# Order of the high-half and low-half products in the feed-forward loop of a two-model transformer kernel

## The chip, the core and the metric

The kernel runs on one core of a Trainium2 chip. The metric is the device time of one execution in microseconds. The median of three runs stands for a kernel. A core has TensorE for matrix products (results go to PSUM, which has eight banks of 512 float32 columns per partition), VectorE, ScalarE, GpSimd, and SyncE, which here issues the loads of the weights.

## What is computed

Two small transformer stacks follow each other on a sequence of 256 tokens with 1024 features. Each has two layers; every layer has a mixer and one or two feed-forward stages. The change lies in the feed-forward stages, of which there are six in all:

```python
def _swiglu(x, wg, wu, wd):
    return (jax.nn.silu(x @ wg) * (x @ wu)) @ wd
...
    for l in range(DEPTH):
        g = norm_g[l]
        h = _swiglu(_rmsnorm(x, g[0]), ffn_w_gate[l, 0], ffn_w_up[l, 0], ffn_w_down[l, 0])
        x = x + 0.5 * _rmsnorm(h, g[1])
...
        h = _swiglu(_rmsnorm(x, g[4]), ffn_w_gate[l, 1], ffn_w_up[l, 1], ffn_w_down[l, 1])
        x = x + 0.5 * _rmsnorm(h, g[5])
```

The weights are float32: gate and up are 1024 x 2816, down is 2816 x 1024. The second stack has one such stage per layer.

## The kernel before

Precision comes from splitting. ScalarE rounds every weight piece (128 x 2048) to a high half `w_hi`, VectorE makes the low half `w_lo = raw - w_hi`, and the activations are split in the same way: `xt[:, kb, 0:256]` is the high half of the transposed input for feature block `kb`, `xt[:, kb, 256:512]` the low half. A product is the sum of three: high by high, high weight by low input, low weight by high input. Because the two halves of `xt` lie side by side, one matmul of 512 columns with a block of `w_hi` standing gives the first two at once, into the two halves of a PSUM bank, and a matmul of 256 columns with `w_lo` standing gives the third, into the first half of the same bank. ScalarE and VectorE add the two halves of the bank afterwards.

A feed-forward stage walks over 11 chunks of 256 hidden features. A chunk has three weight pieces: two for gate and up together (feature blocks 0 to 3 and 4 to 7) and one for down. Each piece lands in one of three slots (`raw`, `w_hi`, `w_lo`), and the slot of a piece is free for the next when the product has used it (`piece_used`).

The first chunk and the last are written out. The eight between run in the hardware loop `with pe.Fori(2, NC - 1, 2) as c`, whose body holds two calls of `step`, so two chunks. One `step` is `gate_up` for chunk c and then `down` for chunk c - 1. In `gate_up` the loop path (no `banks` given) runs over two halves; each half waits once for its piece (`split`) and then goes over four feature blocks `kb`. For one feature block there are four column blocks `b` of 128 (two of gate, two of up), each with its own PSUM bank `GU_LOOP + b`: L1598 is the product of 512 columns, L1601 that of 256. The last instruction of a half raises `piece_used`. `down` is 24 matmuls of 512 columns (L1512, through `threes`).

Around it, a chunk's products are waited for by ScalarE, which copies the second halves of the four banks (L729), and VectorE, which adds the first halves (L1132) and scales the sum (L1136); this frees the banks for the next chunk (`up_scaled`). TensorE runs its instructions in the order in which they are written; no scheduler moves them. Six stages with eight chunks each are 48 passes through a `step`, with 32 matmuls of L1598 and 32 of L1601 in each.

In the profile, a weight load is a row of its own (PEld, LDWEIGHTS) under the line of its matmul.

Of the kernel before, what the change touches and what calls it, by code (L numbers as in the profile page):

```python
# [160 lines left out]
def program(nc, A, out):  # L161
# [5 lines left out]
    with ExitStack() as ctx:  # L167
# [1327 lines left out]
        def _(pe):  # L1495
# [9 lines left out]
            def threes(group, stands="x"):  # L1505

                for n, (hi_lo_a, hi_lo_b) in enumerate(((0, 0), (1, 0), (0, 1))):
                    for o, xh, xl, wh, wl, start, stop in group:
                        a, b = (xh, xl)[hi_lo_a], (wh, wl)[hi_lo_b]
                        if stands == "w":  # L1510
                            a, b = b, a
                        ins = nc.tensor.matmul(o, a, b, start=start and n == 0, stop=stop and n == 2)  # L1512
                return ins

            def split(p, more=0):
                pe.wait_ge(lo_made, p + 1 + more)
# [61 lines left out]
            def ffn(s):  # L1578
                f, p = s["index"], s["piece"]

                def gate_up(q, more=0, banks=None, between=lambda: None):

                    for half in range(2):
                        slot = (q + half) % RING
                        split(q + half, more)
                        for k in range(4):
                            kb = 4 * half + k
                            col = [slice(512 * k + b * P, 512 * k + (b + 1) * P) for b in range(4)]  # L1590
                            if banks:
                                ins = threes([(ps[:, banks[b // 2], (b % 2) * S:(b % 2 + 1) * S],
                                               xt_hi[:, kb, :], xt_lo[:, kb, :], w_hi[slot][:, col[b]],
                                               w_lo[slot][:, col[b]], (kb, b % 2) == (0, 0),
                                               (kb, b % 2) == (KB - 1, 1)) for b in (0, 2, 1, 3)], stands="w")
                                continue
                            for b in range(4):
                                nc.tensor.matmul(ps[:, GU_LOOP + b, :], w_hi[slot][:, col[b]], xt[:, kb, :],  # L1598
                                                 start=kb == 0, stop=False)
                            for b in range(4):  # L1600
                                ins = nc.tensor.matmul(ps[:, GU_LOOP + b, 0:S], w_lo[slot][:, col[b]],  # L1601
                                                       xt_hi[:, kb, :], start=False, stop=kb == KB - 1)
                        ins.then_inc(piece_used, 1)
                        if half == 0:
                            between()
# [17 lines left out]
                def step(c, q, odd, more=0):  # L1623

                    pe.wait_ge(up_scaled, (NC - 1) * f + c - 1)
                    gate_up(q, more)
                    down(c - 1, q + 2, 1 - odd, more)
# [15 lines left out]
                if f == 0:  # L1643
                    pe.wait_ge(consts_made, N_ONES)
                first_product(s, GU_BANKS[0], True)
                gate_up(p + 2, banks=GU_BANKS[1], between=rows_between)
                pe.wait_ge(r_row_made, f + 1)
                down(0, p + 4, 0, start=True)
# [6 lines left out]
                q = p + 3 * NC - 2  # L1655
                pe.wait_ge(up_scaled, (NC - 1) * f + NC - 2)
                gate_up(q - 2, banks=GU_LAST)
                pe.wait_ge(ht_lo_made, f * NC + NC - 1)
                split(q)
# [304 lines left out]
```

## Time and profile before

| What | us |
|---|---|
| median of three runs | 1688.51 |
| lowest and highest | 1686.42 and 1692.31 |
| span of the profiled execution | 1685.5 |
| TensorE matmuls busy | 1583.0 (94% of the span) |
| weight loads busy | 1369.9 (81%) |
| VectorE busy | 1050.5 (62%) |
| ScalarE busy | 825.1 (49%) |

The span is the time between the first and the last instruction in the trace of one execution. The record of a matmul begins when the matmul starts and ends when its result is out, by a model, and the next begins before that, so records overlap: their durations can't be added. How fast matmuls follow each other is the distance between two starts.

### The profile page before, as it was taken

What the parts mean: (1) busy time and instruction counts of PE and PEld (TensorE: products, weight loads), DVE (VectorE), ACT (ScalarE), POOL (GpSimd) and SP (SyncE); (2) the same over time, 40 slices, a digit from 0 to 9 for tenths busy, and PEclk for the clock granted to TensorE, in tenths of its full rate; (3) what the DMA queues carried; (4) which work ended last, traced back from release to release, by engine and by line L of the source; (5) the groups of instructions that cost most, each with busy time, mean ns of one, the idle gap of its engine ahead of it and who ended that gap; (6) DMA issues with size and microseconds to landing.
All of it is one profiled execution on the core that took longest, in us unless ns stands there. A gap on an engine that the chain in (4) does not pass through costs nothing.

```text
span 1685.5 us, 24044 instructions
## 1 busy us (share of the span) xinstructions
PE 1583.0 (94%) x9356; PEld 1369.9 (81%) x9356; DVE 1050.5 (62%) x1242; ACT 825.1 (49%) x985; POOL 40.5 (2%) x63
## 2 busy tenths in 40 slices
PE   7999895899999999999899998989999989799998
PEld 6888794688888888779688887877888879688887
DVE  6566779666667566664566666656666664565665
ACT  5444544555445444544564445544544453644443
POOL 6000000000000000000000000000000000000000
PEclk9999996999999999999999999999999999999999
DMA  8565551265655555554165564545565655155652
GB/s 268 174 206 178 175 147 66 77 223 174 200 174 191 184 192 181 175 176 162 64 206 186 177 207 150 172 129 174 176 200 176 205 175 177 41 174 176 200 176 97
DMA packets 197253, 284.86 MB, mean 169 GB/s; under 512 B 8816, under 2 KB 149136, under 8 KB 197184
## 3 DMA queue, kind: packets, MB, share of 16 engines
q1 hardware_dynamic: 193488, 271.09, 49.1%
q0 software_dynamic: 3552, 12.28, 2.2%
q8 instruction: 49, 0.80, 0.2%
q10 hardware_dynamic: 144, 0.52, 0.1%
q14 instruction: 20, 0.16, 0.0%
HBM read 282.81 MB, written 1.05 MB: 168 GB/s over the span
## 4 chain that ended last, share of the span: by engine, by line
PE 83%; DVE 10%; ACT 5%; issue 2%; DMA 1%; DVEq 0%; POOL 0%; ACTq 0%; POOLq 0%
PE ps L1512 39%; PE ps L1598 21%; PE ps L1601 11%; PE ps L1502 5%; PE ps L1556 2%; DVE mx L1185 2%; DVE w_lo L995 2%; ACT w_hi L625 1%; PE ps L1532 1%; PE ps L1813 1%; DVE shared L1432 1%; DVE xn L1017 1%; DVE xt L1054 1%; ACT junk L660 1%; ACT shared L856 1%
## 5 line engine op out<-in xcount | busy, mean ns | idle before, releaser
L995 DVE TENSOR_TENSOR w_lo<-raw,w_hi 128x2048 fp32r<-128x2048 f32 x257 | 587.8, 2292 | 380.6 <-ACT w_hi L625 380.6
L625 ACT CAST w_hi<-raw 128x2048 fp32r<-128x2048 f32 x257 | 489.5, 1909 | 109.2 <-PE ps L1512 43.7
L1598 PE MATMUL ps<-xt,w_hi 128*128 128x512 f32 x1536 | 418.2, 394 | 0.0
L1598 PEld LDWEIGHTS ps<-xt,w_hi 128*128 128x128 f32 x1536 | 265.9, 189 | 38.2
L1601 PEld LDWEIGHTS ps<-xt,w_lo 128*128 128x128 f32 x1536 | 235.5, 189 | 32.4
L1601 PE MATMUL ps<-xt,w_lo 128*128 128x256 f32 x1536 | 244.1, 281 | 0.0
L1512 PE MATMUL ps<-xt,w_hi 128*128 128x256 f32 x1600 | 227.8, 285 | 3.8 <-DVE w_lo L995 3.4
L1512 PEld LDWEIGHTS ps<-xt,w_hi 128*128 128x128 f32 x1600 | 207.9, 193 | 7.6 <-DVE w_lo L995 6.1
L1512 PE MATMUL ps<-w_hi,ht_hi 128*128 128x512 f32 x528 | 163.9, 391 | 0.0
L1512 PE MATMUL ps<-w_lo,ht_hi 128*128 128x512 f32 x528 | 163.2, 390 | 0.0
L1512 PE MATMUL ps<-w_hi,ht_lo 128*128 128x512 f32 x528 | 163.2, 390 | 0.0
L729 ACT COPY xn<-ps 128x1024 f32<-128x1024 f32 x48 | 48.8, 1017 | 176.8 <-PE ps L1601 176.8
L1512 PE MATMUL ps<-xt,w_lo 128*128 128x256 f32 x800 | 129.8, 284 | 0.0
L1132 DVE TENSOR_TENSOR shared<-ps,xn 128x512 f32<-128x512 f32 x96 | 61.9, 687 | 90.3 <-ACT xn L729 90.3
L723 ACT CAST ht_hi<-shared 128x512 fp32r<-128x512 f32 x60 | 37.4, 623 | 164.4 <-DVE shared L1142 164.4
L1512 PEld LDWEIGHTS ps<-w_hi,ht_lo 128*128 128x128 f32 x528 | 99.1, 188 | 21.9
L1512 PEld LDWEIGHTS ps<-w_lo,ht_hi 128*128 128x128 f32 x528 | 99.1, 188 | 21.2
L1512 PEld LDWEIGHTS ps<-xt,w_lo 128*128 128x128 f32 x800 | 111.2, 193 | 0.0
L731 ACT ACTIVATE shared<-shared 128x512 f32<-128x512 f32 x60 | 38.1, 636 | 145.9 <-DVE shared L1136 95.1
L1512 PEld LDWEIGHTS ps<-w_hi,ht_hi 128*128 128x128 f32 x528 | 94.9, 188 | 16.5
L1502 PE MATMUL ps<-w_hi,xt 128*128 128x512 f32 (+1 forms) x288 | 89.4, 394 | 8.2 <-DVE xt L1453 3.7
L1556 PE MATMUL ps<-w_hi,xt 128*128 128x512 f32 x288 | 78.8, 412 | 4.9 <-issue 2.9
(208 smaller groups left out, 1373.0 us busy)
## 6 DMA issues: line engine op xcount, KB each, us to landing
raw<-in_ffn_w_gate_dram SPq DMA_DIRECT2D x132, 512.0 KB, 3.9
raw<-in_ffn_w_up_dram SPq DMA_DIRECT2D x132, 512.0 KB, 4.9
raw<-in_ffn_w_down_dram SPq DMA_DIRECT2D x132, 512.0 KB, 4.2
raw<-in_fox_w_in_dram SPq DMA_DIRECT2D x24, 512.0 KB, 4.6
raw<-in_a_w_in_dram SPq DMA_DIRECT2D x24, 512.0 KB, 4.6
raw<-in_w_kv_dram SPq DMA_DIRECT2D x16, 512.0 KB, 4.8
raw<-in_ab_w_in_dram SPq DMA_DIRECT2D x14, 512.0 KB, 4.8
gain<-in_norm_g_dram POOLq DMA_DIRECT2D x12, 512.0 KB, 4.0
```

The costliest lines, as they stand in the source:

```text
L625: nc.scalar.copy(w_hi[slot][:, :], raw[slot][:, :]).then_inc(hi_made, 1)
L723: nc.scalar.copy(dst[:, :, :], src).then_inc(ht_hi_made, 1)
L729: nc.scalar.copy(gu_part, ps[:, GU_LOOP:GU_LOOP + 4, S:2 * S]).then_inc(gu_copied, 1)
L731: nc.scalar.activation(sg[:, :, :], sg[:, :, :], ACT.Silu).then_inc(silu_made, 1)
L995: nc.vector.tensor_tensor(w_lo[slot][:, :], raw[slot][:, :], w_hi[slot][:, :].bitcast(F32), ALU.subtract).then_inc(lo_made, 1)
L1132: nc.vector.tensor_tensor(dst[:, :, :], ps[:, two, 0:S], gu_part[:, 2 * n:2 * n + 2, :], ALU.add).then_inc(gu_summed, 1)
L1185: ins = nc.vector.scalar_tensor_tensor(out=acc[:, b, :], in0=a_pad[:, b, j:j + S], scalar=conv_cols[:, b, j:j + 1], in1=acc[:, b, :], op0= ...
L1502: ins = nc.tensor.matmul(o, a, b, start=start and n == 0, stop=stop and n == 2)
L1512: ins = nc.tensor.matmul(o, a, b, start=start and n == 0, stop=stop and n == 2)
L1556: ins = nc.tensor.matmul(o, x_blocks(4 * half + k, t)[part], w[:, 512 * k:512 * (k + 1)], start=start and k == 0, stop=stop and k == 3)
L1598: nc.tensor.matmul(ps[:, GU_LOOP + b, :], w_hi[slot][:, col[b]], xt[:, kb, :], start=kb == 0, stop=False)
L1601: ins = nc.tensor.matmul(ps[:, GU_LOOP + b, 0:S], w_lo[slot][:, col[b]], xt_hi[:, kb, :], start=False, stop=kb == KB - 1)
```

## The change

In `gate_up`, on the path without `banks`, the second loop over the four column blocks is taken out, and its matmul moves into the first loop. The low-half product of a column block now follows the high-half product of the same block at once.

```diff
                             for b in range(4):
                                 nc.tensor.matmul(ps[:, GU_LOOP + b, :], w_hi[slot][:, col[b]], xt[:, kb, :],
                                                  start=kb == 0, stop=False)
-                            for b in range(4):
                                 ins = nc.tensor.matmul(ps[:, GU_LOOP + b, 0:S], w_lo[slot][:, col[b]],
                                                        xt_hi[:, kb, :], start=False, stop=kb == KB - 1)
```

Two places on TensorE show it. The first is the start of the loop body, chunk c: the branch and two register instructions, then the first feature blocks of the first half. `w_hi2` and `w_lo2` are slot 2 of the ring. Before:

```order
L1512 MATMUL ps<-w_lo1,ht_hi0 128x512 x2
L1649 UNCONDITIONAL_BRANCH
L1649 ISA
L1516 ISA
L1598 MATMUL ps<-xt,w_hi2 128x512 x4
L1601 MATMUL ps<-xt,w_lo2 128x256 x4
```

Now, for the first two of the four column blocks (the line numbers behind it are one lower, since a line is gone):

```order
L1512 MATMUL ps<-w_lo1,ht_hi0 128x512 x2
L1648 UNCONDITIONAL_BRANCH
L1648 ISA
L1516 ISA
L1598 MATMUL ps<-xt,w_hi2 128x512
L1600 MATMUL ps<-xt,w_lo2 128x256
L1598 MATMUL ps<-xt,w_hi2 128x512
L1600 MATMUL ps<-xt,w_lo2 128x256
```

Runs of four and four have become single matmuls that alternate. The number in a feature block, four of each, is unchanged.

The second place is the end of the gate/up part, TensorE, where the down part of the chunk before follows (`ht_hi1`, `ht_lo1` are its hidden values, `w_hi1` and `w_lo1` its weights). Before:

```order
L1598 MATMUL ps<-xt,w_hi0 128x512 x4
L1601 MATMUL ps<-xt,w_lo0 128x256 x4
L1516 REGISTER_ALU
L1512 MATMUL ps<-w_hi1,ht_hi1 128x512 x2
L1512 MATMUL ps<-w_hi1,ht_lo1 128x512 x2
L1512 MATMUL ps<-w_lo1,ht_hi1 128x512 x2
```

Now:

```order
L1598 MATMUL ps<-xt,w_hi0 128x512
L1600 MATMUL ps<-xt,w_lo0 128x256
L1516 REGISTER_ALU
L1512 MATMUL ps<-w_hi1,ht_hi1 128x512 x2
L1512 MATMUL ps<-w_hi1,ht_lo1 128x512 x2
L1512 MATMUL ps<-w_lo1,ht_hi1 128x512 x2
```

The down part now stands behind one matmul of 256 columns that itself stands behind one of 512, no longer behind four of 256. The last instruction of the half is the same one.

## Rows read from the trace of the kernel before

**Rows 1.** The page: busy time, granted clock in 40 slices, chain, groups.

```profile
PE 1583.0 (94%) x9356; PEld 1369.9 (81%) x9356; DVE 1050.5 (62%) x1242; ACT 825.1 (49%) x985; POOL 40.5 (2%) x63
...
PEclk9999996999999999999999999999999999999999
...
PE 83%; DVE 10%; ACT 5%; issue 2%; DMA 1%; DVEq 0%; POOL 0%; ACTq 0%; POOLq 0%
PE ps L1512 39%; PE ps L1598 21%; PE ps L1601 11%; PE ps L1502 5%; PE ps L1556 2%; DVE mx L1185 2%; DVE w_lo L995 2%; ACT w_hi L625 1%; PE ps L1532 1%; PE ps L1813 1%; DVE shared L1432 1%; DVE xn L1017 1%; DVE xt L1054 1%; ACT junk L660 1%;
...
L1598 PE MATMUL ps<-xt,w_hi 128*128 128x512 f32 x1536 | 418.2, 394 | 0.0
...
L1601 PE MATMUL ps<-xt,w_lo 128*128 128x256 f32 x1536 | 244.1, 281 | 0.0
```

**Rows 2.** Windows of one chunk: length, busy (count) per engine, clock, DMA share, GB/s.

```profile
62.59:79.28 16.69, 16.69 (x89) 14.31 (x88) 10.48 (x9) 7.38 (x7) 0.00 (x0) 1.00 0.59 190
...
1638.51:1655.20 16.69, 16.69 (x89) 14.32 (x89) 10.48 (x9) 7.80 (x7) 0.00 (x0) 1.00 0.56 189
```

**Rows 3.** Timeline of TensorE, one chunk: start, duration of the group, engine, line.

```profile
62.59 1.07 PE L1598 MATMUL ps<-xt,w_hi 128*128 128x512 f32 x4
63.50 0.64 PE L1601 MATMUL ps<-xt,w_lo 128*128 128x256 f32 x4
63.97 1.09 PE L1598 MATMUL ps<-xt,w_hi 128*128 128x512 f32 x4
64.90 0.63 PE L1601 MATMUL ps<-xt,w_lo 128*128 128x256 f32 x4
65.38 1.09 PE L1598 MATMUL ps<-xt,w_hi 128*128 128x512 f32 x4
...
73.80 0.63 PE L1512 MATMUL ps<-w_hi,ht_hi 128*128 128x512 f32 x2
...
76.11 0.62 PE L1512 MATMUL ps<-w_lo,ht_hi 128*128 128x512 f32 x2
...
79.28 1.07 PE L1598 MATMUL ps<-xt,w_hi 128*128 128x512 f32 x4
```

**Rows 4.** Timeline of TensorE, narrow windows in the next chunk, single starts.

```profile
80.19 0.28 PE L1601 MATMUL ps<-xt,w_lo 128*128 128x256 f32 x1
...
80.30 0.40 PE L1601 MATMUL ps<-xt,w_lo 128*128 128x256 f32 x2
...
80.66 1.09 PE L1598 MATMUL ps<-xt,w_hi 128*128 128x512 f32 x4
...
80.89 0.40 PE L1598 MATMUL ps<-xt,w_hi 128*128 128x512 f32 x1
```

**Rows 5.** Timeline of the weight loads in the chunk of rows 3.

```profile
63.28 0.65 PEld L1601 LDWEIGHTS ps<-xt,w_lo 128*128 128x128 f32 x4
63.86 0.78 PEld L1598 LDWEIGHTS ps<-xt,w_hi 128*128 128x128 f32 x4
```

**Rows 6.** Timeline of TensorE: a stretch of 256 columns only, the down part behind.

```profile
30.44 0.64 PE L1512 MATMUL ps<-xt,w_lo 128*128 128x256 f32 x4
...
33.80 0.38 PE L1634 MATMUL ps<-ident,shared 128*128 128x128 f32 x2
...
40.44 0.63 PE L1512 MATMUL ps<-w_hi,ht_hi 128*128 128x512 f32 x2
...
41.83 0.62 PE L1512 MATMUL ps<-w_hi,ht_hi 128*128 128x512 f32 x2
...
45.91 0.39 PE L1598 MATMUL ps<-xt,w_hi 128*128 128x512 f32 x1
```

**Rows 7.** Timeline of TensorE: matmuls that add into one bank, one after another.

```profile
25.73 1.07 PE L1556 MATMUL ps<-w_lo,xt 128*128 128x512 f32 x4
26.64 0.39 PE L1556 MATMUL ps<-w_hi,xt 128*128 128x512 f32 x1
...
253.42 0.28 PE L1502 MATMUL ps<-xt,w_lo 128*128 128x256 f32 x1
253.54 0.34 PE L1502 MATMUL ps<-w_hi,xt 128*128 128x128 f32 x2
```

**Rows 8.** Timeline of VectorE in the chunk of rows 3, scaling of the sums.

```profile
76.74 1.28 DVE L1136 TENSOR_TENSOR shared<-shared,r_row 128x512 f32<-128x512 f32 x2
```

## The prediction

> **What bounds the kernel now.** I read the page first: TensorE is busy for 1583.0 of 1685.5 us, and 83% of the chain that ended last is on it; the two lines that the change re-orders, L1598 and L1601, hold 21% and 11% of that chain, and no idle time stands before their matmuls [rows 1]. "Busy" says little here, since matmul records overlap, so the quantity to read is the distance from one start to the next. I took it from the timeline of TensorE.
>
> The loop body for one chunk is 64 gate/up matmuls (8 blocks of 4 high and 4 low) and then 24 down matmuls. It takes 16.69 us in the first feed-forward stage and 16.69 us in the last [rows 2], at the full clock of 2.4 GHz (granted 1.00). Eight chunks in each of six stages are 48 bodies, 48 x 16.69 = 801 us, 48% of the span. Since the bodies agree to 0.01 us although DMA and VectorE fall differently, TensorE waits for nobody in them: a nanosecond saved or lost per pair goes into the end time whole, 1536 pairs in all.
>
> The starts give the body's parts [rows 3]. The gate/up part runs from 62.59 to 73.80, 11.21 us; the down part to 79.28, 5.48 us. The first gate/up block takes 63.97 - 62.59 = 1.38 us: high matmuls 0.91 / 4 = 0.2275 us each, low ones 0.47 / 4 = 0.1175 us. The other seven take (73.80 - 63.97) / 7 = 1.404 us; in the second block the four high take 0.93 us and the four low 0.48 us. So a pair now costs 11.21 / 32 = 350.3 ns, 351.1 ns in the seven. Only what lies in these differences can move.
>
> **Settled steps of each length.** In the down part, once settled, 14 matmuls of 512 columns take 79.28 - 76.11 = 3.17 us, 226.4 ns each [rows 3]; in another down part 18 take 45.91 - 41.83 = 4.08 us, 226.7 ns each [rows 6]. In a stretch of 256-column matmuls only, 28 take 33.80 - 30.44 = 3.36 us, 120.0 ns each [rows 6]. A pair made of both settled steps would be 346.7 ns. Each is about 13 ns over its columns at 2.4 GHz (213.3 and 106.7 ns). The rest of today's pair, 351.1 - 346.7 = 4.4 ns, is a price of mixing: high matmuls of blocks 2 to 8 run at 0.93 / 4 = 232.5 ns, not 226.7, with the first one after a low one at 80.89 - 80.66 = 0.23 us [rows 4]. It dies out slowly: after a long run of 256-column matmuls the first six of 512 take 41.83 - 40.44 = 1.39 us instead of 1.36 [rows 6].
>
> **The change, part by part.** Nothing is added or removed: 1536 + 1536 matmuls, as many weight loads, the same semaphore on the last low matmul of each half, the same waits ahead of each half. No DMA is moved past anything.
>
> (a) *Weight loads.* Each matmul has its own load. Loads begin while the matmul before runs: the low loads begin at 63.28, the low matmuls at 63.50; the next high loads at 63.86, their matmuls at 63.97 [rows 5]. The tight place is a load behind a 256-column matmul. There are four in a block today (three low, one high) and four afterwards (all high); the four loose ones behind 512 columns stay four. Count and cover are equal, so the price is 0 if only the neighbour matters. What changes is that no two tight ones follow each other.
>
> (b) *PSUM bank.* Today consecutive matmuls go to different banks; now the low one adds into columns that the high one has just written. The nearest rows are products that add into one bank time after time: 512 on 512 at 26.64 - 25.73 = 0.91 us for four, 227.5 ns each, and 256 on 256 at 253.54 - 253.42 = 0.12 us [rows 7]. Both are the settled steps, so 0, above and below.
>
> (c) *Moving operand.* The high product reads 512 columns of xt and the low one the first 256 of the same; both orders alternate only within that tile. I see no price for it, and bound it by what (d) covers.
>
> (d) *The mix of lengths.* This is the one term that can be other than 0. The lower bound for a pair without a transient is 346.7 ns, the upper one without a new price is 351.1 ns, today's. For the upper end speaks that now every high matmul follows a low one, which is where the slow steps are. For the lower end speaks that the slow steps come after runs of four tight loads, of which none is left. Neither is nearer, so I take the middle, 348.9 ns: 32 x 348.9 = 11.165 us, 0.045 us less per body than 11.21.
>
> (e) *The down part behind it.* Its 24 matmuls would be 24 x 226.7 = 5.44 us settled; 5.48 now, and 5.47 after a long 256-column run (45.91 - 40.44) [rows 6]. After the change the last matmul before is one low behind one high. Between 5.44 and 5.48 I take 5.46, so 0.02 us.
>
> Sum: 48 x (0.045 + 0.02) = 3.1 us less. The profiled execution has a span of 1685.5 us and the median is 1688.5, so 3.0 us lie outside the span; 1685.5 - 3.1 + 3.0 = 1685.4 us.
>
> **Is there cover for a faster TensorE?** What can be late is the next chunk's start, which waits for VectorE's scaled up-product. That ends at 76.74 + 1.28 = 78.02, 1.26 us before the start at 79.28 [rows 8]. This chain starts at the end of the gate/up part, so it is measured against the down part, which shrinks by 0.04 us at most. Nothing new becomes the bound.
>
> The Trainium skill ("TensorE: Matmul & The Clock Gate", Back-to-back issue gap and LDWEIGHTS) gives N/2.4 + 2.5 ns between matmul starts and P/1.2 ns for a weight load. By it a pair would be an estimated 215.8 + 109.2 = 325 ns with the 106.7 ns load just covered in both orders, so the change would be worth nothing; the trace's 351 ns does not agree with its size, but its verdict is the third rival.
>
> **Rivals.**
>
> *Unbroken fast steps.* In a settled state the first low matmul behind a high one is quicker than the others: 80.30 - 80.19 = 0.11 us [rows 4], and in the block at 62.59 the four together take 0.47, so three at 0.12 leave 0.11 [rows 3]. After the change all low matmuls are such first ones. If the settled state is kept, a pair costs 226.7 + 115 = 341.7 ns (0.115 as the cautious reading of rows in steps of 0.01), 10.93 us for 32, 0.28 less, and the down part 0.04 less: 48 x 0.32 = 15.4 us, 1673.1 us. Against it: the step right after that fast one is slow again today, so the state seems to be lost after one low matmul.
>
> *Each change of length costs (slower).* A block today has one turn from low back to high, and costs 1.404 us against 4 x 346.7 = 1.387: 17 ns. If that is the price of the turn, the new order pays it four times: 1.387 + 0.068 = 1.455 us a block, 0.051 more than 1.404; 48 x 8 x 0.051 = 19.6 us, some 1708 us; with half of the price due to the turn (8.5 ns, and 8.5 to the run of low loads that is gone) 1.387 + 0.034 = 1.421 and 6.5 us, 1695 us. It makes the kernel measurably slower once a pair exceeds 351.1 + 3.3 = 354.4 ns. Against it: the excess isn't at the turn, it is spread over the four high matmuls, and one turn into the long down part costs 0.03 to 0.04 us, not more than its first steps.
>
> *The order doesn't matter.* The 13 ns over the columns and the 4.4 ns on top are paid per instruction in this mix, whatever stands where: 351.1 ns a pair, 1688.5 us.
>
> **How the numbers follow.** A measurement of this kernel can tell about 0.3%, 5.1 us, from no change. The forecast case (346.7 to 351.1 ns, 7.6 us less to 0, so 1681 to 1688.5) gets 0.55, of which 0.20 is faster by more than that. Unbroken fast steps get 0.17, all faster. The order doesn't matter: 0.13. A price per turn: 0.15, of which 0.02 within 0.3%. Of the forecast case, 0.02 is left for slower, 0.33 for within. Faster: 0.20 + 0.17 = 0.37. Within: 0.33 + 0.13 + 0.02 = 0.48. Slower: 0.13 + 0.02 = 0.15. The range reaches from 1669 (the fast-step case with 0.113 us, which rows rounded to 0.01 us allow too: 48 x 0.38 = 18 us less, and a little) to 1699 (half of the turn's price, and a little); outside it lies the full price of the turn, about 1 in 10, and little below.
>
> **What would show it.** In the changed trace the body should take 16.62 us, between 16.53 and 16.69, the same in all 48; a pair should take 349 ns, high about 230 and low about 119. Low steps of 113 to 115 ns with high ones at 227 mean the first rival, high steps near 240 the second. Records of 0.23 and 0.12 with idle time between would mean a wait that I have missed, in the first place on VectorE's scaling ahead of a chunk. I am wrong in kind if the pair leaves 341 to 354 ns, or if any body differs from the others.

## The result, and the profile after

The changed kernel takes 1692.87 us (median of 20 runs, 1687.13 to 1694.71) against 1688.68 us (20 runs) before. The ratio is 1.0026, with a 95% interval from 1.0018 to 1.0035: slower by a quarter of a per cent. That is inside the 0.3% which the prediction called "within", and inside its range, but on the other side of no change from the forecast of 3.1 us less.

The page of the changed kernel, lines that answer to [rows 1]:

```profile
PE 1587.9 (94%) x9356; PEld 1370.4 (81%) x9356; DVE 1050.7 (62%) x1242; ACT 823.1 (49%) x985; POOL 40.6 (2%) x63
...
PE 83%; DVE 9%; ACT 5%; issue 2%; DMA 1%; DVEq 0%; POOL 0%; ACTq 0%; POOLq 0%
...
L1598 PE MATMUL ps<-xt,w_hi 128*128 128x512 f32 x1536 | 544.1, 398 | 0.0
...
L1600 PE MATMUL ps<-xt,w_lo 128*128 128x256 f32 x1536 | 431.3, 281 | 0.0
```

The chain's shares by engine are the same but for VectorE (10% before, 9% now), and no idle time stands before either matmul. Two traps are in these lines. The busy time of L1598 went from 418.2 to 544.1 us and that of L1601 (now L1600) from 244.1 to 431.3, which is not work. The busy time of a line counts a stretch once in which its own records overlap. Now a record of the other line stands between two of one line: two of L1598 start 353 ns apart and last 398, so they overlap by 45 ns only; those of L1600 (281 ns) don't overlap each other at all. The mean record of L1598 went from 394 to 398 ns; its end is by a model, so the steps from start to start below are the measure.

Windows of one loop body, in the first stage and in the last, as in [rows 2]:

```profile
62.99:79.79 16.80, 16.80 (x90) 14.31 (x88) 10.48 (x9) 7.36 (x7) 0.00 (x0) 1.00 0.59 188
...
1643.97:1660.77 16.80, 16.80 (x90) 14.30 (x88) 10.48 (x9) 7.79 (x7) 0.00 (x0) 1.00 0.56 187
```

The windows have 16.69 and 16.80 us; the trace, which keeps starts in whole nanoseconds, has 16.687 before and 16.793 after, each the same within 1 ns in all 48 bodies. Over all bodies the difference is 0.107 us a body, 48 x 0.107 = 5.1 us of the 5.5 us between the two spans (1691.0 and 1685.5). The other 0.4 us lies outside the bodies, where nothing was changed.

The timeline of TensorE in one body (start, duration of the group, line), to be read beside [rows 3]:

```profile
62.99 0.39 PE L1598 MATMUL ps<-xt,w_hi 128*128 128x512 f32 x1
63.22 0.28 PE L1600 MATMUL ps<-xt,w_lo 128*128 128x256 f32 x1
63.34 0.40 PE L1598 MATMUL ps<-xt,w_hi 128*128 128x512 f32 x1
63.57 0.28 PE L1600 MATMUL ps<-xt,w_lo 128*128 128x256 f32 x1
63.69 0.40 PE L1598 MATMUL ps<-xt,w_hi 128*128 128x512 f32 x1
63.93 0.28 PE L1600 MATMUL ps<-xt,w_lo 128*128 128x256 f32 x1
...
67.58 0.40 PE L1598 MATMUL ps<-xt,w_hi 128*128 128x512 f32 x1
...
74.28 0.64 PE L1512 MATMUL ps<-w_hi,ht_hi 128*128 128x512 f32 x2
...
77.52 0.62 PE L1512 MATMUL ps<-w_hi,ht_lo 128*128 128x512 f32 x2
...
79.79 0.39 PE L1598 MATMUL ps<-xt,w_hi 128*128 128x512 f32 x1
```

The first pair takes 0.34 us to the nanosecond. From 63.34 to 67.58 there are twelve pairs in 4.24 us, 353.3 ns each. The gate/up part takes 74.28 - 62.99 = 11.29 us and the down part 79.79 - 74.28 = 5.51 us. To the nanosecond the two parts are 11.290 and 5.503 us, against 11.200 and 5.487 before: the prediction's 11.21 and 5.48 came from starts rounded to 0.01 us, and so did its pair of 351.1 ns in the seven later blocks, which is 350.8.

The steps from start to start in nanoseconds, from the same two traces (h high, l low, d down), show what sums hide:

```
before   h226 h227 h227 h226 l114 l119 l120 l120 | h233 h236 h228 h233 l117 l120 l117 l117 | h235 h233 h236 h224 l118 l120 l120 l120 | ...
         d235 d233 d236 d224 d231 d236 d228 d233 d230 d227 d227 ...
changed  h227 l113 h233 l117 h241 l120 h236 l113 | h233 l117 h241 l120 h236 l113 h233 l117 | ...
         d241 d238 d233 d236 d224 d231 d236 d228 d233 d230 d227 ...
```

From body to body a single step differs by about 1 ns, as starts are whole nanoseconds. The changed kernel runs through a cycle of three pairs: 233 + 117, 241 + 120, 236 + 113, which is 1060 ns or 353.3 a pair. The fast low step of 113 ns is there, in every third pair; it is paid for by a high step of 232 to 241 ns behind each low one, where 227 would be the settled one.

### The profile page after: what moved, and what is told of

Same layout as the page of the kernel before. It is cut to its first block, busy times and chain, and to the rows that moved or that the text cites. A ratio compares the mean times of both kernels' runs of the same rounds, so it can differ in the third digit from the quotient of the medians.

```text
span 1691.0 us, 24044 instructions
## 1 busy us (share of the span) xinstructions
PE 1587.9 (94%) x9356; PEld 1370.4 (81%) x9356; DVE 1050.7 (62%) x1242; ACT 823.1 (49%) x985; POOL 40.6 (2%) x63
## 4 chain that ended last, share of the span: by engine, by line
PE 83%; DVE 9%; ACT 5%; issue 2%; DMA 1%; DVEq 0%; POOL 0%; ACTq 0%; POOLq 0%
PE ps L1512 39%; PE ps L1598 21%; PE ps L1600 11%; PE ps L1502 5%; PE ps L1556 3%; DVE mx L1185 2%; DVE w_lo L995 2%; PE ps L1532 1%; ACT w_hi L625 1%; PE ps L1812 1%; DVE shared L1432 1%; DVE xn L1017 1%; ACT shared L856 1%; DMA gain<-in_norm_g_dram 1%; ACT junk L660 0%
## 5 line engine op out<-in xcount | busy, mean ns | idle before, releaser
L1598 PE MATMUL ps<-xt,w_hi 128*128 128x512 f32 x1536 | 544.1, 398 | 0.0
L1600 PE MATMUL ps<-xt,w_lo 128*128 128x256 f32 x1536 | 431.3, 281 | 0.0
L1598 PEld LDWEIGHTS ps<-xt,w_hi 128*128 128x128 f32 x1536 | 288.6, 188 | 71.3
L1600 PEld LDWEIGHTS ps<-xt,w_lo 128*128 128x128 f32 x1536 | 290.0, 189 | 1.9
L1512 PEld LDWEIGHTS ps<-xt,w_hi 128*128 128x128 f32 x1600 | 208.0, 193 | 7.6 <-DVE w_lo L995 6.1
L1512 PE MATMUL ps<-xt,w_lo 128*128 128x256 f32 x800 | 129.8, 284 | 0.0
L1512 PEld LDWEIGHTS ps<-xt,w_lo 128*128 128x128 f32 x800 | 111.2, 193 | 0.0
```

## Experiments

Two theories stood at first. "Lengths": a step is only settled (226.7 or 120.0 ns) among steps of its own length, and a change of length unsettles the ones behind it. "Bank": it costs to add into the PSUM bank that the matmul before has just written. A third, "loads", took the reason in the weight load that just fits behind a 256-column matmul. All kernels change only the loop of L1597 to L1602 and compute the same sums unless said. Only one_turn and pairs_2_2 were run often enough (seven times) for their whole time to tell a few us; the others ran once, and what is compared of them is the body in the trace, which doesn't vary.

**Another bank.** Each low product is held back by one, so that it never goes to the bank just written:

```diff
...
                             for b in range(4):
...
+                                if late:
+                                    c, kc, cols = late
+                                    ins = nc.tensor.matmul(ps[:, GU_LOOP + c, 0:S], w_lo[slot][:, cols],
+                                                           xt_hi[:, kc, :], start=False, stop=kc == KB - 1)
+                                late = (b, kb, col[b])
+                            if k == 3:
...
```

The last low one of a half has no high one left to wait for and follows at once (`if k == 3`).

> High and low products alternate one by one as in the changed kernel, but each low one is held back by one, so it goes to the bank of the column block before, never to the bank just written. Loop body before: 16.69 us; changed: 16.79 us (trace). Theory 'lengths' (alternating 512 and 256 columns keeps the array out of its settled step, whatever the bank): 16.79 us, within 0.02. Rival 'bank' (adding into the bank just written costs): 16.69 us or less. Theory 'loads' (see alt_384) expects what 'lengths' does here.

The timeline of TensorE: the body's start, two starts three pairs apart, the down part, the next body's start.

```profile
62.73 0.62 PE L1600 MATMUL ps<-xt,w_hi 128*128 128x512 f32 x2
...
63.30 0.40 PE L1600 MATMUL ps<-xt,w_hi 128*128 128x512 f32 x1
...
64.36 0.40 PE L1600 MATMUL ps<-xt,w_hi 128*128 128x512 f32 x1
...
74.02 0.63 PE L1512 MATMUL ps<-w_hi,ht_hi 128*128 128x512 f32 x2
...
79.48 0.39 PE L1600 MATMUL ps<-xt,w_hi 128*128 128x512 f32 x1
```

Three pairs take 1.06 us, the very cycle of the changed kernel (the steps read h233 l117 h241 l120 h236 l113). "Bank" falls. The body, 79.48 - 62.73 = 16.75 us, is 0.04 below the 16.79 expected, outside the 0.02 allowed. All of it is in the down part, 79.48 - 74.02 = 5.46 us against 5.51; the gate/up part is 11.29 us in both. Here two low products stand together at the end of each half, and only two steps behind them are slow (d236 d233 d227).

**Two and two.** Two high, two low, in each feature block twice:

```diff
-                            for b in range(4):
...
+                            for two in ((0, 1), (2, 3)):
+                                for b in two:
...
+                                for b in two:
...
```

> Two high, two low, two high, two low: two turns from low to high in a feature block instead of one (before) or four (changed); never two products in one bank in a row. 'Lengths' and 'loads', if the price goes with the number of turns: 16.69 + 0.106 / 3 = 16.72 us per body. 'Bank': 16.69 us. If the price is not by turns but by the length of the low run, it can be anywhere from 16.6 to 16.8.

> The kernel of pairs_2_2 again, now timed: its body took 16.587 us in the trace against 16.687, so 48 x 0.100 = 4.8 us (0.28%) less is expected, ratio 0.997.

```profile
62.70 0.61 PE L1599 MATMUL ps<-xt,w_hi 128*128 128x512 f32 x2
...
64.08 0.63 PE L1599 MATMUL ps<-xt,w_hi 128*128 128x512 f32 x2
...
65.47 0.63 PE L1599 MATMUL ps<-xt,w_hi 128*128 128x512 f32 x2
...
73.83 0.63 PE L1512 MATMUL ps<-w_hi,ht_hi 128*128 128x512 f32 x2
...
79.28 0.39 PE L1599 MATMUL ps<-xt,w_hi 128*128 128x512 f32 x1
```

This is the timeline of the run pairs_2_2_timed; the block between 64.08 and 65.47 takes 1.39 us against 1.403 before, and the body 79.28 - 62.70 = 16.58 us (16.587 in the trace). The expectation by the number of turns, 16.72, was wrong: twice the turns of the kernel before cost less than its turns do. The median of seven runs is 1680.76 us against 1686.96 for the kernel before (thirteen runs beside them), ratio 0.9965 (0.9953 to 0.9977), in line with 48 x 0.100 = 4.8 us.

**Equal lengths.** The order of the changed kernel, with the low product over all 512 columns:

```diff
-                                 ins = nc.tensor.matmul(ps[:, GU_LOOP + b, 0:S], w_lo[slot][:, col[b]],
-                                                        xt_hi[:, kb, :], start=False, stop=kb == KB - 1)
+                                 ins = nc.tensor.matmul(ps[:, GU_LOOP + b, 0:2 * S], w_lo[slot][:, col[b]],
+                                                        xt[:, kb, :], start=False, stop=kb == KB - 1)
```

> Alternation of the changed kernel, but the low-half product also has 512 columns (it adds the low-by-low product as well, which the kernel before leaves out). Same alternation of weight tile and same bank twice in a row, but equal lengths. 'Lengths' and 'loads': every step settled, 88 x 226.7 = 19.95 us per body. 'Bank': 32 pairs with 3 to 6 ns more, 20.05 to 20.15 us.

```profile
66.19 0.39 PE L1598 MATMUL ps<-xt,w_hi 128*128 128x512 f32 x1
...
68.00 0.39 PE L1598 MATMUL ps<-xt,w_hi 128*128 128x512 f32 x1
...
86.13 0.39 PE L1598 MATMUL ps<-xt,w_hi 128*128 128x512 f32 x1
```

Four pairs in 68.00 - 66.19 = 1.81 us, 226 ns a step; the body is 86.13 - 66.19 = 19.94 us (19.947 in the trace), and all 88 steps are 226 or 227 ns. Alternating the weight tile and using one bank twice cost nothing, not a nanosecond.

**A length without a tight load.** The same with 384 columns (`0:S + P`), so that a load has some 173 ns to fit in and not 120:

> Alternation of the changed kernel with a low-half product of 384 columns (it adds the low-by-low product for half of the tokens, which the kernel before leaves out). Lengths still differ, but no weight load is tight any more (steps of 109 to 120 ns are the least seen between loads, a 384-column step is about 173). 'Loads' (the unrest comes from a load that just fits behind a 256-column matmul): settled, 32 x (226.7 + 173.3) + 24 x 226.7 = 18.24 us per body. 'Lengths' (any change of length unsettles): 18.24 + 32 x 0.0064 = 18.44 us.

```profile
64.52 0.39 PE L1598 MATMUL ps<-xt,w_hi 128*128 128x512 f32 x1
...
64.91 0.39 PE L1598 MATMUL ps<-xt,w_hi 128*128 128x512 f32 x1
...
66.13 0.40 PE L1598 MATMUL ps<-xt,w_hi 128*128 128x512 f32 x1
...
82.97 0.39 PE L1598 MATMUL ps<-xt,w_hi 128*128 128x512 f32 x1
```

Three pairs take 66.13 - 64.91 = 1.22 us, 406.7 ns each; the body is 18.45 us. That is the value of "lengths", 18.44, and "loads" (18.24) falls. The settled step of 384 columns, 173.3 ns, is an estimate from those of 256 and 512, but the high steps show it without that: they are 231 to 233 ns here, not 227. With the estimate the excess is 6.7 ns a pair, as in the changed kernel: 353.3 - 346.7 = 6.6 ns.

**Long runs.** If unequal neighbours are what costs, few and long runs should be cheapest. Eight high and eight low, sixteen and sixteen, and, as the fewest turns there can be, this:

```diff
...
+                            order = ("hl", "lh")[half]
+                            for part in order:
+                                for kb, b in itertools.product(range(4 * half, 4 * half + 4), range(4)):
...
+                                    if part == "h":
+                                        ins = nc.tensor.matmul(ps[:, GU_LOOP + b, :], w_hi[slot][:, cols],
+                                                               xt[:, kb, :], start=kb == 0, stop=last)
+                                    else:
+                                        ins = nc.tensor.matmul(ps[:, GU_LOOP + b, 0:S], w_lo[slot][:, cols],
+                                                               xt_hi[:, kb, :], start=False, stop=last)
...
```

> Eight high, then eight low (two feature blocks together): four turns from low to high in a body. 'Lengths' with a price per turn of 10 to 46 ns, less 7 for the first low one: 16.533 + 4 x (0.003 to 0.039) = 16.55 to 16.69 us, nearer to the upper end if a turn costs what it costs after runs of four. 'Two is special': 16.69 us.

> 16 high, then 16 low in each half: two turns from low to high in a body. 'Lengths': 16.533 - 2 x 0.007 + 2 x (0.010 to 0.046) = 16.54 to 16.61 us. 'Two is special': 16.65 to 16.69 us.

> First half: 16 high, then 16 low products; second half: 16 low, then 16 high. With the down part of 24 around it, a body has one turn from high to low and one from low to high. 'Lengths': all steps settled is 56 x 226.7 + 32 x 120 = 16.53 us; the first low one gives back 7 ns, the one turn back costs 10 to 46 ns (what the down parts of the runs so far show over 24 x 226.7): 16.54 to 16.57 us per body against 16.69 before, so 5.5 to 7.3 us less. Rival 'two is special' (the gain of pairs_2_2 comes from its pattern of two and long runs are like runs of four): 16.65 to 16.69 us, no more than 2 us less.

The timeline of the last one, a whole body with the down part behind 74.44:

```profile
63.33 3.79 PE L1605 MATMUL ps<-xt,w_hi 128*128 128x512 f32 x16
66.96 4.00 PE L1608 MATMUL ps<-xt,w_lo 128*128 128x256 f32 x32
70.79 3.82 PE L1605 MATMUL ps<-xt,w_hi 128*128 128x512 f32 x16
74.44 0.61 PE L1512 MATMUL ps<-w_hi,ht_hi 128*128 128x512 f32 x2
...
79.88 0.39 PE L1605 MATMUL ps<-xt,w_hi 128*128 128x512 f32 x1
```

Sixteen high products take 66.96 - 63.33 = 3.63 us when settled and 74.44 - 70.79 = 3.65 us behind the low ones. The down part is 5.44 us, all settled, and the body 79.88 - 63.33 = 16.55 us. The median of seven runs is 1679.71 us against 1686.96, ratio 0.9961 (0.9947 to 0.9974): it is faster than the kernel before, by what its bodies give (48 x 0.133 = 6.4 us). The changed kernel wasn't run beside it; through the kernel before, which both were compared with, one_turn is faster than that too. With pairs_2_2 it is level within the intervals.

The bodies of the other two (start and next start), with the first runs of eight:

```profile
62.52 1.98 PE L1603 MATMUL ps<-xt,w_hi 128*128 128x512 f32 x8
64.33 1.12 PE L1606 MATMUL ps<-xt,w_lo 128*128 128x256 f32 x8
65.28 2.00 PE L1603 MATMUL ps<-xt,w_hi 128*128 128x512 f32 x8
67.13 1.11 PE L1606 MATMUL ps<-xt,w_lo 128*128 128x256 f32 x8
...
73.67 0.63 PE L1512 MATMUL ps<-w_hi,ht_hi 128*128 128x512 f32 x2
...
79.13 0.39 PE L1603 MATMUL ps<-xt,w_hi 128*128 128x512 f32 x1
```

```profile
62.35 3.79 PE L1604 MATMUL ps<-xt,w_hi 128*128 128x512 f32 x16
...
78.92 0.39 PE L1604 MATMUL ps<-xt,w_hi 128*128 128x512 f32 x1
```

16.61 us with runs of eight, 16.57 with runs of sixteen. "Two is special, long runs are like runs of four" (16.65 and more) falls for both. The down part of the first, 79.13 - 73.67 = 5.46 us (5.467 in the trace), is 27 ns over settled; its steps are d234 d236 d228 d232 d231 d227, though it reads another tile (`ht`) than the low products before it.

**Lone low runs.** What does a low run of n leave behind, if the high ones before it and after it have time to settle? In each half: 8 high, n low, 8 high, the rest low, with n = 1 and 2 in one kernel, 3 and 4 in the other:

```diff
...
+                            todo = {part: list(itertools.product(range(4 * half, 4 * half + 4), range(4))) for part in "hl"}
+                            for part, count in ((("h", 8), ("l", 1), ("h", 8), ("l", 15)),
+                                                (("h", 8), ("l", 2), ("h", 8), ("l", 14)))[half]:
+                                for kb, b in [todo[part].pop(0) for _ in range(count)]:
...
```

> The same 64 products in runs of 8 high, 1 low, 8 high, 15 low (first half) and 8 high, 2 low, 8 high, 14 low (second). It shows what one low product, and two, leave behind among settled high ones. If a single low one is the dearest and two are cheap (as pairs_2_2 hints, 3 ns per turn against 8 in the changed kernel): after one, some 10 slow high steps and 40 ns; after two, 2 slow ones and under 15 ns. Rival: every low run, short or long, leaves the same 27 ns in five high steps (as runs_8, runs_16 and one_turn show for long ones), and the low turn price of pairs_2_2 comes only from cutting the recovery off. Body: 16.533 - 4 x 0.007 + 2 x 0.027 for the long ones + what the short ones cost.

> As lone_1_2, with lone runs of three and of four low products. Four should leave what long runs leave, 27 ns in five steps (a run of four between runs of four high ones costs 20 net in the kernel before). Three tells whether the price depends on odd and even or falls and rises with the length: 27 ns if it is the same for all, more if odd ones are dear.

The timelines, n = 1 and 2:

```profile
62.69 1.98 PE L1605 MATMUL ps<-xt,w_hi 128*128 128x512 f32 x8
64.50 0.28 PE L1608 MATMUL ps<-xt,w_lo 128*128 128x256 f32 x1
64.62 2.00 PE L1605 MATMUL ps<-xt,w_hi 128*128 128x512 f32 x8
66.46 1.96 PE L1608 MATMUL ps<-xt,w_lo 128*128 128x256 f32 x15
...
70.32 2.00 PE L1605 MATMUL ps<-xt,w_hi 128*128 128x512 f32 x8
72.17 1.83 PE L1608 MATMUL ps<-xt,w_lo 128*128 128x256 f32 x14
```

and n = 3 and 4:

```profile
64.72 2.00 PE L1605 MATMUL ps<-xt,w_hi 128*128 128x512 f32 x8
66.56 1.72 PE L1608 MATMUL ps<-xt,w_lo 128*128 128x256 f32 x13
...
70.43 2.00 PE L1605 MATMUL ps<-xt,w_hi 128*128 128x512 f32 x8
72.27 1.59 PE L1608 MATMUL ps<-xt,w_lo 128*128 128x256 f32 x12
```

Settled, eight high ones take 64.50 - 62.69 = 1.81 us. Behind one low they take 66.46 - 64.62 = 1.84, behind two 1.85, behind three 1.84, behind four 1.84. The steps are the same in all: h233 h236 h228 h232 h231, then h227, which is 27 ns over five settled steps (233 is 232 behind a single low one). My own guess, that one is dearest and two are cheap, fell; its rival, the same 27 ns for every low run, stands.

**All bodies side by side.** All settled steps would sum to 32 x 346.67 = 11.093 us in the gate/up part, 24 x 226.67 = 5.440 in the down part, 16.533 together. The body is the mean over all 48, and the last column has the medians of whole kernels, with the kernel before that ran beside them in brackets.

| Order in the gate/up part | turns low to high per body | gate/up, us | down, us | body, us | over 16.533, ns | mean per turn, ns | whole kernel, us |
|---|---|---|---|---|---|---|---|
| one_turn | 1 | 11.113 | 5.440 | 16.553 | 20 | 20 | 1679.71 (1686.96) |
| runs_16 | 2 | 11.106 | 5.467 | 16.573 | 40 | 20 | one run, 1682.66 (1686.96) |
| runs_8 | 4 | 11.146 | 5.467 | 16.613 | 80 | 20 | one run, 1686.55 (1686.96) |
| lone_1_2, lone_3_4 | 4 | 11.146 | 5.467 | 16.613 | 80 | 20 | one run each, 1686.87, 1683.22 (one, 1688.40) |
| before (4 and 4) | 8 | 11.200 | 5.487 | 16.687 | 153 | 19 | 1688.68 |
| pairs_2_2 | 16 | 11.137 | 5.450 | 16.587 | 53 | 3 | 1680.76 (1686.96) |
| other_bank (1 and 1) | 30 | 11.291 | 5.456 | 16.747 | 213 | 7 | one run, 1687.24 (one, 1686.46) |
| changed (1 and 1) | 32 | 11.290 | 5.503 | 16.793 | 260 | 8 | 1692.87 (1688.68) |

equal_512 (1844.58 us) and alt_384 (1770.05), one run each, do more work and are not in the table.

A turn costs 27 ns in the five high steps behind it and the low run gives back 7 at its start (113 instead of 120): 20 net, wherever at least eight high ones stand on either side of the low run. The 19 of the kernel before is a mean of two prices. A turn inside the gate/up part has only four high ones behind it, and each block after the first takes 16 ns more than its settled steps. The last turn, into the down part, costs 47 ns in nine steps (d235 to d230 above). So a recovery that the next low run cuts off isn't simply shortened: by these steps part of it comes later, behind the low run. With one or two high steps between low runs the mean price is 8 or 3 ns a turn. So the change made four times as many turns at two fifths of the price, and the excess went from 153 to 260 ns per body.

## Why the prediction was wrong

**The bound, and where the time would appear: right.** TensorE alone carries the bodies, and what a body gains or loses goes into the end: 0.107 x 48 = 5.1 us in the bodies, 4.2 us between the medians, 5.5 us between the spans. The chain ahead of a chunk did not become late; all bodies stayed equal.

**(a) Weight loads at 0: right, as far as the runs tell.** The alternation with equal lengths ran at settled steps with as many loads, and alt_384 showed that the excess doesn't need a tight load: it is 6.7 ns a pair without one and 6.6 with one.

**(b) Bank and (c) moving operand at 0: right for the bank, shown; for the operand as far as the rows tell.** other_bank has the same cycle in other banks, and equal_512 is settled in the same bank. It read 512 columns for both products, so it can't part a price for reading half of the same tile from a price for the unequal length. But the price of a turn doesn't need one tile read twice: the long 256-column run in [rows 6] is followed by the down part, which reads another tile, and the steps from 40.44 on are 234, 236, 228, 232, 231 and then 227 ns, the five slow steps of every lone turn. The trace of the kernel before had them already.

**(d) The mix of lengths: the step that failed.** It was bounded by 346.7 and 351.1 ns, the upper one being today's "without a new price", and the middle, 348.9, was taken. A pair costs 353.3 ns, beyond the upper end. The bound was no bound: today's price of mixing was measured with one turn in eight matmuls, and nothing said that four turns could not cost more. The argument for the upper end (every high matmul now follows a low one, where the slow steps are) was the right one. The one for the lower end, that slow steps come after runs of four, is refuted by lone_1_2: one low product unsettles as much as fifteen. In the sum it is +0.090 us per body (11.200 to 11.290) instead of -0.045.

**(e) The down part: wrong by the same cause.** 5.503 us instead of 5.46, and 0.017 more than before instead of 0.02 less. Behind the alternation it takes ten steps until they are settled, where it took nine (the list of steps above). The prediction took it for granted that one low product behind one high one would leave no more than a run of four does. How the alternation ends counts as well: other_bank has the same cycle but ends on two low ones, and its down part takes 5.456 us. Why is not shown.

**Its own signs.** The prediction set the body between 16.53 and 16.69 us, and it takes 16.79. High steps were to be about 230 ns, or near 240 for the second rival: their mean in the cycle is 236.7 (233, 241, 236), between the two. A pair of 353.3 ns stays just inside the 341 to 354 beyond which it would have called itself wrong in kind, so that limit was too wide to catch this.

**The rivals.** The second, each change of length costs, had the right sign and the right mechanism, with a price of 17 ns per turn, or half. That is the price of a turn in blocks of four (16 to the nanosecond); that the 20 ns of a lone turn lie near it is in part chance, since the one is a recovery cut off and the other a whole one. What the rival lacked is that closer turns cost less each: its full price gave +0.41 us per body, half of it +0.136, and it was +0.107. The argument held against it, that the excess is spread over the four high matmuls, was no argument: a turn's price is spread over five steps. The first rival's fast low steps exist (113 ns) but only in the first pair of a body and in every third behind it, and only in that first pair with a settled high step beside them. The third, that order doesn't matter, is refuted by the table: the same 88 matmuls of one body took from 16.553 to 16.793 us. The formula that the Trainium skill gives ("TensorE: Matmul & The Clock Gate", Back-to-back issue gap) depends on the column count alone, so it can't tell these orders apart; the section itself calls it the gap of an isolated matmul and says that in a stream of weight loads and matmuls both set the spacing.

## What to carry to other kernels

When TensorE is the bound, find the places where short matmuls turn into long ones, and read the steps from start to start there one by one; busy times and means of a line say nothing about it. Put products of one length next to each other in long runs, across feature blocks and across the halves of a stage if the data are there. The number of turns alone forecasts nothing once turns are close: fewest turns (one_turn, 1) and two by two (16) were both some 0.4% faster than four by four (8), and one by one (32) was the slowest. And a bound taken from today's order is not a bound for another order; it needs a row in which that order, or a piece of it, has run.

## What the runs showed of the hardware that was not expected

- A turn from 256 to 512 columns (products of fp32r data, granted clock 1.00) leaves 27 ns in the next five matmuls, as 233 (232 behind a single short one), 236, 228, 232, 231 ns against 227. It was the same for every length of the short run that was tried between long runs of eight or more: 1 to 4, 8, 12 to 16 and 32. It repeats within a nanosecond in all 48 bodies.
- In runs of four and four the five slow steps are cut off after four, and four short matmuls don't wipe out the rest: the next four long ones take 235, 233, 236, 224 ns, and the long run behind the last block needs nine steps.
- Alternating one by one never settles. With 512 and 256 columns it is a cycle of three pairs (353.3 ns each on average). With 512 and 384 the long steps are 231 to 233 ns (about 407 ns a pair). With 512 and 512 it is settled from the first step.
- From 256 to 512 columns the settled step grows by 106.7 ns (120.0 to 226.7), 2.4 columns per ns; that leaves 13.3 ns in either step that don't go with the columns. Why, and what is unsettled by a change of length, stays open: the runs exclude the bank, a tight load as its condition and a wait for another engine, and name no part. Why turns behind two high steps cost 3 ns and behind one 8 ns is open too; no order was tried that would tell.
